# Hybrid decoder layer on one core: compressed scores in row pairs, recurrence output later, dilated rows normalised first, last squares on ScalarE, last gate tile in halves

## The reference, cut to what matters

```python
s_c = einsum('bkgqd,bknd->bkgqn', qi, k_cmp) - sl * abs(tf - cmp_ctr)      # compressed keys
p_c, _ = _softmax_masked(s_c, cmp_end <= t)
o = gi0 * (p_c @ v_cmp) + gi1 * o_s + gi2 * o_w                            # six NSA heads
outs[g] * softmax(stack(lses))[g]                                          # six dilated heads
o = o * rsqrt(mean(o*o) + EPS) * silu(g)                                   # four HGRN2 heads
h = h + _rmsnorm(concat([o_nsa, o_dil, o_hg]) @ w_out)
h = h + _rmsnorm(square(relu(_rmsnorm(h) @ w_up)) @ w_down)
h = h + (p @ w_ple_proj) * sigmoid(_rmsnorm(h) @ w_ple_gate)
```

## Time and profile before

| | us |
|---|---|
| median of 3 runs | 769.27 (768.45 to 770.61) |
| the profiled execution, its own time | 768.97 |
| its span in the trace | 767.2 |
| TensorE busy in it | 740.7 |
| VectorE, ScalarE, GpSimd busy | 391.3, 321.8, 13.6 |
| mean granted clock of TensorE | 0.978 of 2.4 GHz |

### The profile page before, as it was taken

How to read it: one execution, slowest core, us unless ns; L and a number is a source line. 1 busy time by engine, 2 the same in 40 slices (tenths; PEclk the granted TensorE clock), 3 DMA queues, 4 the chain that set the end, 5 groups by cost and what they waited for, 6 DMA issues and landing times.

```text
span 767.2 us, 10439 instructions
## 1 busy us (share of the span) xinstructions
PE 740.7 (97%) x4230; PEld 600.1 (78%) x4230; DVE 391.3 (51%) x617; ACT 321.8 (42%) x505; POOL 13.6 (2%) x20
## 2 busy tenths in 40 slices
PE   6999999989999997999999999999999999999897
PEld 5889888778865563887888888888888888888686
DVE  3588754355245646137554434534453444549634
ACT  6655543742355656225623213241323313234631
POOL 2000000000000200000100000000000000000000
PEclk9999999986999999999999999999999999999899
DMA  9514323410110101351331332222322332223102
GB/s 348 213 28 166 114 107 111 165 56 1 56 55 1 56 1 60 115 211 56 105 114 56 110 111 89 93 92 109 103 94 76 109 109 62 104 108 110 55 14 97
DMA packets 12406, 73.67 MB, mean 96 GB/s; under 512 B 1552, under 2 KB 2352, under 8 KB 4688
## 3 DMA queue, kind: packets, MB, share of 16 engines
q1 hardware_dynamic: 11968, 70.03, 25.4%
q0 software_dynamic: 256, 3.11, 1.0%
q10 hardware_dynamic: 144, 0.00, 0.0%
HBM read 70.51 MB, written 2.10 MB: 95 GB/s over the span
## 4 chain that ended last, share of the span: by engine, by line
PE 89%; DVE 4%; ACT 2%; issue 2%; DMA 1%; SPq 0%; DVEq 0%; ACTq 0%
PE bank L1293 27%; PE bank L1294 26%; PE bank L1295 26%; PE bank L1609 2%; PE bank L1473 2%; PE bank L1596 2%; PE bank L1570 1%; DMA raw<-wst 1%; PE bank L1404 1%; ACT Whi L593 1%; DVE Wlo L892 1%; DVE arena L1265 1%; PE bank L1490 1%; PE bank L1613 1%; PE bank L1454 0%
## 5 line engine op out<-in xcount | busy, mean ns | idle before, releaser
L1293 PE MATMUL bank<-Xhi,Whi 128*128 128x512 f32 x472 | 186.6, 395 | 1.6 <-DVE Xlo L937 0.7
L1295 PE MATMUL bank<-Xhi,Wlo 128*128 128x512 f32 x472 | 184.7, 391 | 0.0
L1294 PE MATMUL bank<-Xlo,Whi 128*128 128x512 f32 x472 | 184.6, 391 | 0.0
L892 DVE TENSOR_TENSOR Wlo<-raw,Whi 128x2048 fp32r<-128x2048 f32 x53 | 121.4, 2291 | 88.3 <-ACT Whi L593 88.3
L593 ACT ACTIVATE Whi<-raw 128x2048 fp32r<-128x2048 f32 x54 | 103.2, 1912 | 139.6 <-PE bank L1295 130.7
L1293 PE MATMUL bank<-Whi,Uhi 128*128 128x512 f32 (+1 forms) x328 | 126.0, 384 | 0.0
L1294 PE MATMUL bank<-Wlo,Uhi 128*128 128x512 f32 (+1 forms) x328 | 124.7, 380 | 0.0
L1295 PE MATMUL bank<-Whi,Ulo 128*128 128x512 f32 (+1 forms) x328 | 124.4, 379 | 0.0
L1293 PEld LDWEIGHTS bank<-Xhi,Whi 128*128 128x128 f32 x472 | 89.1, 189 | 25.4 <-issue 6.4
L1295 PEld LDWEIGHTS bank<-Xhi,Wlo 128*128 128x128 f32 x472 | 89.1, 189 | 18.9
L1294 PEld LDWEIGHTS bank<-Xlo,Whi 128*128 128x128 f32 x472 | 89.3, 189 | 17.7
(11 more groups left out here) (211 smaller groups left out, 725.8 us busy)
## 6 DMA issues: line engine op xcount, KB each, us to landing
raw<-wst SPq DMA_DIRECT2D x59, 1024.0 KB, 4.8
arena<-ctab POOLq DMA_DIRECT2D x1, 2880.0 KB, 11.5
arena<-xn SPq DMA_DIRECT2D x4, 512.0 KB, 5.8
arena<-xn SPq DMA_DIRECT2D x1, 2048.0 KB, 7.9
out<-arena SPq DMA_DIRECT2D x8, 256.0 KB, 2.0
arena<-gpost SPq DMA_DIRECT2D x2, 512.0 KB, 9.6
arena<-arena SPq DMA_DIRECT2D x8, 64.0 KB, 2.0
arena<-lmask SPq DMA_DIRECT2D x1, 224.0 KB, 10.9
```

The lines of the kernel that those rows point to most:

```text
L892: nc.vector.tensor_tensor(Wlo[:, g % 2, :], raw[:, g % 2, :], Whi[:, g % 2, :].bitcast(fp32), ALU.subtract).then_inc(lo_done, 1)
L1293: mm(out_ap, w[0], x[0], start=start, stop=False, **kw)
L1294: mm(out_ap, w[0], x[1], start=False, stop=False, **kw)
L1295: return mm(out_ap, w[1], x[0], start=False, stop=stop, **kw)
```

## The change

- `cmp_scores` takes k = 0 and k = 1 by turns, so that successive matmuls use different halves of the rows. The addition of the distances becomes `cmp_distance`, with a semaphore `cs_add` of its own, ahead of `normalise` in step 3. V3 and the value products wait for `cs_add` in place of `cs_ev`. The exponential moves to step 4 on ScalarE, `cmp_weights` to step 6.
- The split of panel 15 moves from step 1 to step 2, `hg_out` and its `Uhi` copies to step 4, `hg_lo` to step 5. In step 1 `normalise` comes ahead of `cmp_keys`.
- From step 24 on `normalise(u - 1)` comes ahead of unit u's rows.
- ScalarE splits panel 19 at the start of step 27 in place of its end, and GpSimd, no longer VectorE, takes its lower part. VectorE waits for that before its part of panel 20.
- `near_values(0)` and `(1)` move ahead of the transposes of the last unit and wait for `s_ev` 54.
- In the last eighth of the MLP ScalarE squares, too.
- The last gate tile (tokens 384 to 511, columns 512 to 1023) is computed in two column halves, in bank `QB[7]` and, once its sigmoid has read it, `QB[0]`; sigmoid, product, addition and output follow by halves.

The diff, with eight columns of indentation left out:

```diff
@@ -281,6 +281,7 @@
 cs_mm = sem("cs_mm")
+cs_add = sem("cs_add")
 cs_ev = sem("cs_ev")
@@ -483,6 +484,9 @@
+ENDS = [(n % TT, slice(n // TT * 512, (n // TT + 1) * 512), QB[n][:, :]) for n in range(7)]
+ENDS += [(3, slice(512 + 256 * a, 768 + 256 * a), QB[(7, 0)[a]][:, 0:256]) for a in range(2)]
+
 LAST = ((0, 0), (0, 1), (0, 2), (1, 0), (1, 1), (0, 3), (1, 2), (1, 3))
@@ -536,12 +540,10 @@
         load_panel(g)
-    for n in range(8):
+    for n, (t, c, _) in enumerate(ENDS):
         sp.wait_ge(o_done, n + 1)
-        t, nh = n % TT, n // TT
-        sp.dma_start(out[t * P:(t + 1) * P, nh * 512:(nh + 1) * 512],
-                     H[:, t, nh * 512:(nh + 1) * 512]).then_inc(out_sent, 16)
-    sp.wait_ge(out_sent, 128)
+        sp.dma_start(out[t * P:(t + 1) * P, c], H[:, t, c]).then_inc(out_sent, 16)
+    sp.wait_ge(out_sent, 16 * len(ENDS))
@@ -571,6 +573,9 @@
     nc.gpsimd.tensor_tensor(Wlo[:, G_PLE % 2, :], raw[:, G_PLE % 2, :], Whi[:, G_PLE % 2, :].bitcast(fp32),
+                            ALU.subtract).then_inc(lo_done, 1)
+    pool.wait_ge(hi_done, G_OUT + 1)
+    nc.gpsimd.tensor_tensor(Wlo[:, G_OUT % 2, :], raw[:, G_OUT % 2, :], Whi[:, G_OUT % 2, :].bitcast(fp32),
                             ALU.subtract).then_inc(lo_done, 1)
@@ -726,6 +731,8 @@
                         product_copy(n)
+                if u == NA - 1:
+                    hi(G_OUT)
                 if u < NA:
@@ -734,12 +741,7 @@
                                              accum_out=den[:, n:n + 1]).then_inc(p_exp, 1)
-                if u == 2:
-                    for j in range(2):
-                        act.wait_ge(oh_done, 1)
-                        nc.scalar.activation(Uhi[:, 3 + j, :], tD[:, j * SEQ:(j + 1) * SEQ],
-                                             ACT.Copy).then_inc(mix_hi, 1)
-                if u == C_SCORES:
+                if u == C_SCORES + 1:
                     act.wait_ge(cs_ev, 1)
@@ -756,10 +758,15 @@
                     product_copy(n)
-                if u in (NA - 1, NA):
-                    hi(G_OUT + u - NA + 1)
-                if u == 1:
+                if u == NA:
+                    hi(G_OUT + 1)
+                if u == 2:
                     hi(15)
+                if u == 4:
+                    for j in range(2):
+                        act.wait_ge(oh_done, 1)
+                        nc.scalar.activation(Uhi[:, 3 + j, :], tD[:, j * SEQ:(j + 1) * SEQ],
+                                             ACT.Copy).then_inc(mix_hi, 1)
                 for g in range(14, G_PT):
@@ -837,6 +844,10 @@
                         nc.scalar.activation(relu[:, f % 2, :], bank[:, :], ACT.Relu).then_inc(up_relu, 1)
+                        if last and e == 1:
+                            act.wait_ge(up_relu, i * 8 + u + 1)
+                            act.wait_ge(up_lo, i * 8 + u - 1)
+                            nc.scalar.activation(usq[:, f % 2, :], relu[:, f % 2, :], ACT.Square).then_inc(up_sq, 1)
                         act.wait_ge(up_sq, i * 8 + u + 1)
@@ -869,13 +880,12 @@
     act.wait_ge(h_rs, 2)
-    for n in range(8):
+    for n, (t, c, bank) in enumerate(ENDS):
         act.wait_ge(gt_mm, n + 1)
         if n >= 4:
             act.wait_ge(o_done, n - 3)
-
-        nc.scalar.activation(Gsig[:, n % 4, :], QB[n][:, :], ACT.Sigmoid,
-                             scale=rs_h[:, TT + n % TT:TT + n % TT + 1]).then_inc(gt_sig, 1)
+        nc.scalar.activation(Gsig[:, n % 4, 0:c.stop - c.start], bank, ACT.Sigmoid,
+                             scale=rs_h[:, TT + t:TT + t + 1]).then_inc(gt_sig, 1)
@@ -1053,11 +1063,14 @@
-            def cmp_arguments():
+            def cmp_distance():
                 for k in range(NKV):
                     dve.wait_ge(cs_mm, k + 1)
-                    link(V2.tensor_tensor(PC[:, k * 384:(k + 1) * 384], PB[(OB, FB)[k]][:, 0:384], ctb[:, k, :],
-                                          ALU.add))
+                    V2.tensor_tensor(PC[:, k * 384:(k + 1) * 384], PB[(OB, FB)[k]][:, 0:384], ctb[:, k, :],
+                                     ALU.add).then_inc(cs_add, 1)
+
+            def cmp_arguments():
+                dve.wait_ge(cs_add, 2)
                 link(V2.tensor_reduce(cst, pc3, AX.X, ALU.min))
@@ -1119,6 +1132,8 @@
             for u in range(NA + 2):
+                if NU <= u <= NA:
+                    normalise(u - 1)
                 if NU <= u < NA:
@@ -1133,21 +1148,24 @@
                                                 accum_out=mneg[:, n:n + 1]).then_inc(s_ev, 1)
+                if u == C_SCORES:
+                    cmp_distance()
+                if u == 5:
+                    hg_lo()
+                if 1 <= u < NU:
+                    normalise(u - 1)
                 if u == 1:
                     cmp_keys()
-                if 1 <= u <= NA:
-                    normalise(u - 1)
-                if u == 2:
-                    hg_out()
-                if u == 3:
-                    hg_lo()
                 if u == C_SCORES:
                     cmp_arguments()
-                if u == C_SCORES + 1:
+                if u == 4:
+                    hg_out()
+                if u == 6:
                     cmp_weights()
-                if u in (NA - 1, NA):
-                    lo(G_OUT + u - NA + 1)
-                if u == 1:
+                if u == NA:
+                    dve.wait_ge(lo_done, G_OUT + 1)
+                    lo(G_OUT + 1)
+                if u == 2:
                     lo(15)
@@ -1211,11 +1229,12 @@
                         u = 4 * e + f
-                        dve.wait_ge(up_relu, i * 8 + u + 1)
-                        if u:
-                            dve.wait_ge(up_lo, i * 8 + u)
-                        V2.tensor_tensor(usq[:, f % 2, :], relu[:, f % 2, :], relu[:, f % 2, :],
-                                         ALU.mult).then_inc(up_sq, 1)
+                        if not (last and e == 1):
+                            dve.wait_ge(up_relu, i * 8 + u + 1)
+                            if u:
+                                dve.wait_ge(up_lo, i * 8 + u)
+                            V2.tensor_tensor(usq[:, f % 2, :], relu[:, f % 2, :], relu[:, f % 2, :],
+                                             ALU.mult).then_inc(up_sq, 1)
                         dve.wait_ge(up_hi, i * 8 + u + 1)
@@ -1276,12 +1295,11 @@
         gate_lo(c)
-    for n in range(8):
-        t, nh = n % TT, n // TT
+    for n, (t, c, _) in enumerate(ENDS):
+        sig = Gsig[:, n % 4, 0:c.stop - c.start]
         dve.wait_ge(gt_sig, n + 1)
-        link(V2.tensor_tensor(Gsig[:, n % 4, :], Gsig[:, n % 4, :], PR[:, t, nh * 512:(nh + 1) * 512], ALU.mult))
-        hv = H[:, t, nh * 512:(nh + 1) * 512]
-        V2.tensor_tensor(hv, hv, Gsig[:, n % 4, :], ALU.add).then_inc(o_done, 1)
+        link(V2.tensor_tensor(sig, sig, PR[:, t, c], ALU.mult))
+        V2.tensor_tensor(H[:, t, c], H[:, t, c], sig, ALU.add).then_inc(o_done, 1)
@@ -1506,6 +1524,7 @@
                 pe.wait_ge(t_ev, NKV * (NU + i + 1))
+                pe.wait_ge(s_ev, NKV * (NA - 1))
                 for blk in (1, 0)[:i + 1]:
@@ -1528,7 +1547,7 @@
                 if u == V_FOURTH:
-                    pe.wait_ge(cs_ev, 1)
+                    pe.wait_ge(cs_add, 2)
                 for n, k in fill_of[u]:
@@ -1562,14 +1581,15 @@
                 pe.wait_ge(job_evac, V_JOBS[V_AT[2]] + 1)
-                for k in range(NKV):
-                    r = slice(k * HD, (k + 1) * HD)
-                    for i in range(TT):
-                        for g in range(NG):
-                            o = (i * NG + g) * NCP
+                for i in range(TT):
+                    for g in range(NG):
+                        o = (i * NG + g) * NCP
+                        for k in range(NKV):
+                            r = slice(k * HD, (k + 1) * HD)
                             last = mm(PB[(OB, FB)[k]][:, o:o + NCP], T[r, Q0 + g, i * P:(i + 1) * P], kcT[r, :],
                                       start=True, stop=True)
-                    last.then_inc(cs_mm, 1)
+                            if i == TT - 1 and g == NG - 1:
+                                last.then_inc(cs_mm, 1)
@@ -1629,14 +1649,15 @@
                     turn_cmp()
+                if u == NA + 1:
+                    near_values(0)
+                    near_values(1)
                 if u >= 2:
...
                     values(*pieces(u))
-            near_values(0)
-            near_values(1)
             near_values(2)
@@ -1726,6 +1747,18 @@
         for t in range(TT):
+            if nh and t == TT - 1:
+                pe.wait_ge(gt_sig, 1)
+                for a, bank in enumerate((QB[7], QB[0])):
+                    for k in range(4):
+                        x = tuple(gate_x(b, 4 * kh + k)[:, t * P:(t + 1) * P] for b in (Whi, Wlo))
+                        w = tuple(b[:, 4 * (c % 2) + k, 256 * a:256 * a + 256] for b in (Xhi, Xlo))
```

(6 more changed lines are left out.)

## The result

| | before | after |
|---|---|---|
| median | 769.78 (768.45 to 770.61, 4 runs) | 759.24 (758.47 to 760.09, 4 runs) |
| ratio, 95% interval | | 0.9865 (0.9846 to 0.9884) |
| span of the profiled execution | 767.2 | 756.6 |
| mean granted clock | 0.978 | 0.989 |
| TensorE busy | 740.7 | 731.9 |

The change gains 10.5 us, 1.35%. The forecast of 762.0 was 2.8 too high, within its own 759.5 to 764 but for 0.3, and the range held it.

What follows compares the result with a forecast made beforehand. TensorE, busy for 97% of the span, bounds the kernel: only its list, waits and clock count. 8.3 - 1.5 + 0.5 = 7.3 us gained, so 762.0; forecast 759.5 to 764, range 755.5 to 766.5.

Steps and rivals of the forecast that it cites:

- First term: Compressed scores up to V5: earlier start, records by turns and moved work bring V5 8.3 us earlier.
- The upper bound for V3: Compressed scores: V3 starts at 171.5, after VectorE's distance additions, hiding a score length up to about 5 us.
- I take half of the 0.200: Compressed scores: two array halves share the records, so each takes half its 0.200 us, 4.8 us for 48.
- Second term: Last dilated softmax units: GpSimd's split holds the last unit's row minimum on VectorE; a loss of 1.5 us.
- I take 1.2 later and 0.3 for a longer slow stretch: Dilated units: w_out starts 1.2 us later than 308.57, plus 0.3 for more time at 1.2 GHz.
- Last eighth: Last eighth of the MLP: squares moved to ScalarE change nothing, within 0.2 us either way.
- Last gate tile: End of the kernel: two column halves cost 0.3 us of matmuls, save 0.8 behind them; net 0.5 gained.
- The first: Dilated units: GpSimd holds only the TENSOR_SCALARs, not the row minimum; say 4 us gained, time 756.5, chance 0.30.
- The second: Compressed scores: turns don't pay; the gain there is 5.2 or 3.4 us, time 765 to 767, chance 0.13.
- The third: Compressed scores: switching halves makes every record wait for the last; scores last 19 us, time 776, chance 0.03.
- The fourth: Whole kernel: the waits move on further than followed and nothing is left, time 769, chance 0.04.

Runs made afterwards that it cites:

- e1: The kernel before with only the order of the compressed scores' records changed, k = 0 and k = 1 by turns; 766.56 us, ratio 0.9962.
- a0: The changed kernel run again unaltered, as reference for its group of runs; 758.81 us, ratio 0.9864 to the kernel before.
- e3: The changed kernel with panel 19's lower part split by VectorE after the last unit's normalising, not by GpSimd; 754.8 us, ratio 0.9804.
- e6: The changed kernel with the last unit's row minimum written as a TENSOR_SCALAR, GpSimd's split kept; 754.61 us, ratio 0.9808.
- e7: The kernel before with only the dilated part: normalising first, panel 19 split early and by GpSimd, near_values earlier; 766.59 us, ratio 0.9987.
- e5: The changed kernel with the squares of the MLP's last eighth back on VectorE; 759.26 us, ratio 0.9862.
- e2: The changed kernel with the old score loop, all of k = 0 and then all of k = 1; 760.36 us, ratio 0.9895.

## Why the prediction was right

**The bound and the place.** It held that only TensorE's waits, list and clock count, and that the compressed scores were the main place. 8.9 of the 10.6 us lie there. Some 4 of them are clock under the records, which the forecast did not tell apart from turns.

**First term, 8.3 forecast, 8.9 measured.** Point by point, forecast and trace: scores from 165.5 (165.19), VectorE's split until 169.6 (169.52), V3 at 171.5 (171.19), V4 at 178.1 (178.04), V5 at 185.9 (185.15). The upper bound for V3 was VectorE, as stated. Two steps were off. The length of the scores, "I take half of the 0.200", was too high: 4.8 forecast, 2.77 measured. The half was right (e1: 4.77 at nearly the old clock), but the scores now run at 2.4 GHz, since they end before the clock falls, and there it is 0.058. It was hidden, as the prediction said of anything up to 5 us, and cost nothing. The other is V5: between V4's start and V5's I summed records on ScalarE at full length, 0.9 + 1.15 + 1.91. In the trace one record starts 0.1 before the last ends (177.44, 178.18 and 179.23 for 0.85 and 1.15). The same overlap in the exponentials ahead of them had already let V3's copy end at 177.54 and not 178.1, and ScalarE's split of panel 16 ended at 181.14, not at 182.1. In a0, where V4 started by ScalarE's copy, V4 to V5 is 7.3 against 7.8 forecast. TensorE itself takes 7.1 from V4 to V5 as before (178.04 to 185.15), and this is what set V5 in the profiled execution. V4's agreement is partly luck: the forecast had ScalarE's copy set it at 178.1, in the execution that copy was out at 177.54, and V4 followed TensorE's own work, since V3 happened to run at 1.2 GHz. In a0 the copy did set V4, 17.0 after V2 against 17.3 forecast.

**Second term, 1.5 lost forecast, 0.3 gained measured.** Its mechanism was right down to the instruction: L1131 held until GpSimd ends, TensorE's wait 5.45, the transposes 3.5 later than they would come (forecast 3.7); e3 and e6 each undo it and each gain 4. By the Trainium skill (SBUF — State Buffer, "Who interferes with whom") a VectorE instruction with two SBUF inputs contends with a GpSimd instruction that reads SBUF; the traces agree, down to a tile of 128 x 1 (3.72 for 0.16). In e6 the same minimum with one tensor and one scalar operand was not held (0.21), while the TENSOR_SCALAR of 512 columns, with one tensor operand too, was (3.70), so the number of tensor inputs alone does not decide. `w_out` started at 300.31, 8.26 earlier than before; 8.3 less the 1.2 for its start made it 7.1. What failed is the step "I take 1.2 later and 0.3 for a longer slow stretch". Taking the 9.0 by which V5's row moved off, `w_out` lost 0.8, close to the 1.0 of the waits. The clock, which was put at 1.3 more (1.0 of the 1.2, and the 0.3), gave back about as much as the waits cost: the slow stretch was as long, 6.8, but TensorE worked through 4.93 of it and not 6.80, so (6.80 - 4.93)/2 = 0.9 less was lost. Before, another 2.5 us at 1.2 GHz lay just ahead of the gate, after only 0.2; TensorE waits for 0.6 longer there in exchange (1.00 for 0.38 at the gate's first matmul). By the gate, the part stands at 0.3 gained. By these figures the gain is the clock's, which differs between executions, and e7 shows no gain of the part that can be told.

**Last eighth: nothing.** So it was (e5). **Last gate tile: 0.5 forecast**, 0.7 at full clock. The other 0.5 of the gate's 1.2 is the clock: 4.4 us at 1.2 GHz before, 3.3 after, which no step of the forecast had.

**The rivals.** The first (L1131 not held, 756.5) fell, and e6, where it holds by construction, ran in 754.6. The second (turns don't pay) fell in its reason, the records do halve, but the first term hangs on turns even less than its price says: without them the kernel is 1.5 slower by the medians (e2) and level at equal clock, not 3 to 5 slower, because V3 waits for VectorE. The third, a serial switch of the halves, is excluded by 0.058. The fourth too.

**The sum.** 8.9 + 0.3 + 1.2 + 0.2 = 10.6 against 7.3: 0.6 more in the first term, 1.8 more around `w_out`, most of it clock, 0.7 at the gate (clock and a last tile sized low), 0.2 before V2.

## What to carry to other kernels

When work is handed to GpSimd, look at which VectorE instruction first meets it and who waits for that one: here a minimum over one column, 0.16 us long, was held for 3.72 and cost 4 us, and writing it with a scalar operand, or leaving the split on VectorE, gave these 4 us back, where the offload itself gave nothing that can be told (e7). When an engine becomes the one that is late, list what its own first instruction waits for: moving back only ScalarE's half of the split brought 2.2 us in the trace. When a stretch at 1.2 GHz moves or shrinks together with a change, say which part of the gain is clock before the edit gets the credit. And sum a busy engine by the distance from start to start, not by the length of its records.

## What the runs showed of the hardware

- Float32 records of 64 x 128 stationary and 32 moving columns, all in one half of the rows and one bank, come every 0.213 at 1.2 GHz (before) and every 0.112 at 2.4 GHz (e2, until 169.95). By turns two of them come in the time of one: a pair every 0.213 at 1.2 GHz (e1) and every 0.112 at 2.4 GHz (after). Whether the other half or the other bank does it is not separated.
- The 256-column matmuls of V4 to V7, with stationary rows at a stride of four, come every 0.233 at 1.2 and at 2.4 GHz alike (a0); those of V3 every 0.213 and 0.120.
- During GpSimd's 128 x 2048 subtraction (4.50 to 4.57) VectorE's TENSOR_TENSOR of 128 x 1 took 3.72, a TENSOR_SCALAR of 128 x 1 with its scalar in SBUF 0.21, and a TENSOR_SCALAR of 128 x 512 3.70. The held ones end within 0.3 of GpSimd (290.40 for 290.38 in after, 291.08 for 290.79 in e6).
- GpSimd takes 4.50 for what VectorE does in 2.29.
- The place of the stretches at 1.2 GHz differs between executions of one kernel. In the kernel after, one execution had 0.50 from 171.2 to 177.3, a0 had 1.00 from 171.8 to 177.5:

```profile
171.80:177.50 5.70, 4.21 (x34) 3.85 (x34) 5.49 (x16) 1.99 (x6) 0.00 (x0) 1.00 0.42 170
```

  The parts that TensorE alone sets differ by up to 3 us with it (48.6 to 51.4 from the gate to the end, last tile in halves), so a part worth under a microsecond has to be read at equal clock.
